# Picking the first group's rows in two parts in a transformer layer with a mixture of experts

## The chip, the cores and the metric

The kernel runs on one core of one Trainium2 chip. The metric is the time of one execution on the device in microseconds (us), as the median of several runs. The core has five engines that run their own instruction lists and wait for one another by semaphores: TensorE (PE in the profile; PEld is its loading of stationary operands), VectorE (DVE), ScalarE (ACT), GpSimd (POOL) and SyncE (SP), which here issues nearly all DMAs. A profiler on the chip records every instruction; the "granted clock" of TensorE is given as a share of its full 2.4 GHz.

## What is computed

One transformer layer on 512 rows (tokens) of 2048 features: a norm, one wide projection, three kinds of attention, an output projection added to the input, and then a mixture of experts with two levels of routing, whose output is added and normed. All is float32. The part that matters here:

```
xt = h.reshape(N, D)                                   # N = 512, D = 2048
g_prob = softmax(xt @ wg + bg); g_p, g_idx = top_k(g_prob, 1)          # one of 8 groups
e_in = the 8 expert logits of the row's own group
e_val, e_loc = top_k(e_in, 2)                          # two of its 8 experts
weight = g_p * softmax(e_val)
y[row] = sum over its two experts e of
         weight * ((silu(x @ w_gate[e]) * (x @ w_up[e])) @ w_down[e])
```

There are 64 experts, each with three matrices of 2 MB (2048x256, 2048x256, 256x2048), 403 MB in all, which are read once.

## The kernel before

Up to about 970 us the kernel does the norm, the projection and the attentions; then comes the output projection, which leaves the layer's rows in the chip's memory and, as a copy, in DRAM. From there on it goes through the 8 groups one after the other, and in each group through its 8 experts (`group(c, g, ...)`, one function of this name for each engine, with the same loop).

**Routing, ahead of the first group (lines 1209 to 1278 and 2114 to 2188).** TensorE computes the router's logits, VectorE finds each row's group and its two experts. TensorE helps with small products: a running count of the rows of each group (L1258), the rows' places in their group (`place_rows`, L1230), a running count of the chosen rows of each expert (L1270), and the slot of each row (`place_slots`, L1237). Each is followed by a step of VectorE that the next one waits for. Between them `keep_busy(n)` (L1252) runs n products of 128x128 whose result nobody reads; each shows as two records, as all float32 products do. One of these calls has n = 16 and stands ahead of the wait for the chosen experts (`chosen_ready`).

**Rows of a group and slots of an expert.** A group's rows (at most 128) are gathered by GpSimd with an indirect DMA into `xg` (two buffers). An expert has 64 slots (`CAP`). `pick` is a matrix of 128 rows by 8*64 slots that holds a 1 where row r sits in slot s of expert e; VectorE builds it in one step by comparing each row's slots with a count (`build_pick`, L2182).

**The pick.** The products of an expert need its rows turned, features by slots. That is done for four experts at a time (a half of the group, 256 columns): for each of the 16 pieces of 128 features one product of `xg` with `pick` (`pick_half`, L1297) leaves 128 features x 256 slots in a bank of the accumulator memory (PSUM), and ScalarE (even pieces, L1733) or VectorE (odd pieces, L2202) copies it to `xT`, times the norm's factor `ln2`. There are four places in PSUM for this, used in turn (`TURN4`); a pick waits until the last content of its place has been copied out. Group 0's first half is picked right after the routing, its second half after expert 3's gate and up, and the halves of later groups likewise.

**An expert.** `gate_up` multiplies its slots with the gate and up matrices, 16 pieces each, side by side in the array (L1375 and L1376), into one of two banks in turn (bank 7, `PJ`, and bank 6). Ahead of the first expert of a group it also makes eight small products with the same bank, which bring each slot's factor of the norm (the "root products", L1367). ScalarE takes the silu of the gate's half (L1753), VectorE multiplies by the up half (L2257), TensorE turns the result (L1385), and `down_product` multiplies it with the down matrix (L1400); the results are spread back over the group's rows (L1346). TensorE does this in the order: gate and up of expert e, then turn, spread and down of expert e-1. In group 0, after expert 0's gate and up, stands `place_marks` (L1245), which prepares the spreading.

**Loads.** SP issues the weights in a fixed order (`LOAD_ORDER`) into 8 slots of 2 MB. A load waits until the last user of its slot is done: `gu_done` counts experts whose gate and up are done, `down_done` those whose down product is done. The loads that follow experts 0 and 1 into their slots are cut into quarters (`load_quarters`, L753): after each quarter of gate and up TensorE signals `quarter_used`, and 2 x 512 KB go out; the fourth quarter waits for `gu_done`. Two more loads (half a matrix each, L798) wait for the gather of group 0's rows, because they overwrite the place of the rows that it reads beside.

## Time and profile before

| | us |
|---|---|
| median of 3 timed runs | 1949.46 (1948.17 to 1949.99) |
| the profiled execution's own time | 1948.38 |
| its span, first to last instruction | 1946.6 |
| TensorE busy in the span | 1871.2 (96%) |
| VectorE, ScalarE, GpSimd busy | 705.6, 584.6, 245.3 |
| DMA, all queues | 505.95 MB, mean 260 GB/s |
| mean granted clock | 0.991 |

The profile cuts the span into 40 slices of 48.7 us. TensorE shows as busy in nearly all of them, but a busy TensorE is not one at its peak, since the matmuls are pipelined and their ends modelled. The rate of the transfers has two levels: it varies between 44 and 349 GB/s up to the twenty-first slice, and is even from there on. Which of the two sets the pace of a stretch has to be read from that stretch.

### The profile page before, as it was taken

How to read it: one execution, taken by the hardware profiler on the slowest of the kernel's cores; microseconds unless marked ns; L12 is line 12 of the kernel's file. 1: busy time of each engine (PE TensorE's matmuls, PEld its weight loads, DVE VectorE, ACT ScalarE, POOL GpSimd, SP SyncE). 2: the span in 40 equal slices, each digit the busy share in tenths (PEclk: the TensorE clock that was granted, in tenths of full speed). 3: DMA queues.
4: the chain of work that ended last, by engine and by line, in shares of the span. 5: the costliest groups of instructions: out<-in, count | busy, mean ns of one | idle time of the engine just before them, and what ended most of it. 6: DMA issues, size and time to landing. Idle time of an engine off the chain costs nothing.

```text
span 1946.6 us, 28605 instructions
## 1 busy us (share of the span) xinstructions
PE 1871.2 (96%) x11936; PEld 1352.2 (69%) x11936; DVE 705.6 (36%) x1773; ACT 584.6 (30%) x1212; POOL 245.3 (13%) x208
## 2 busy tenths in 40 slices
PE   6999999999999999999999999989999899999997
PEld 6887777777777767788986666556665565656663
DVE  5331223333766668701042232322323222222222
ACT  5323333333443444422312232212212122121322
POOL 2433343433000000144100000000000000000000
PEclk9999999999999999999999999999999999999999
DMA  9554233234232232145489999999999999999995
GB/s 284 134 147 118 66 86 82 70 71 92 45 76 44 55 117 79 44 142 195 191 349 420 429 426 426 427 427 427 427 426 427 427 428 426 428 427 427 427 423 231
DMA packets 177745, 505.95 MB, mean 260 GB/s; under 512 B 52930, under 2 KB 136258, under 8 KB 151754
## 3 DMA queue, kind: packets, MB, share of 16 engines
q1 hardware_dynamic: 175306, 495.66, 66.5%
q0 software_dynamic: 2304, 8.39, 1.1%
q8 instruction: 97, 1.59, 0.3%
q14 instruction: 38, 0.31, 0.1%
HBM read 495.88 MB, written 16.53 MB: 263 GB/s over the span
## 4 chain that ended last, share of the span: by engine, by line
PE 81%; DMA 16%; ACT 1%; DVE 1%; issue 0%; SPq 0%; POOL 0%; POOLq 0%; ACTq 0%; DVEq 0%
PE banks L967 26%; PE banks L1375 13%; PE banks L1124 9%; PE banks L1400 8%; DMA x_region<-in_w_up 7%; DMA at_region<-in_w_up 7%; PE banks L1297 6%; PE banks L1376 3%; PE banks L1104 3%; PE banks L1076 2%; PE banks L1054 2%; PE banks L1346 2%; DMA ht_region<-in_w_up 2%; PE banks L1016 1%; PE banks L1215 1%; PE banks L1061 1%
## 5 line engine op out<-in xcount | busy, mean ns | idle before, releaser
L967 PE MATMUL banks<-ht_rounded,ring_rounded 128*128 128x512 f32 x1056 | 359.2, 394 | 0.7 <-ACT at_region L1538 0.7
L967 PEld LDWEIGHTS banks<-ht_rounded,ring_rounded 128*128 128x128 f32 x1056 | 195.1, 188 | 53.3 <-issue 13.8
L1375 PE MATMUL banks<-at_region,ht_region 128*64 128x256 f32 x800 | 179.0, 382 | 9.3 <-DMA at_region<-in_w_up 9.3
L864 POOL TENSOR_TENSOR ring_rounded<-ring_region,at_rounded 128x512 fp32r<-128x512 f32 (+1 forms) x92 | 115.9, 1291 | 511.3 <-ACT at_rounded L1477 511.3
L1376 PE MATMUL banks<-at_region,ht_region 128*64 128x256 f32 x768 | 175.3, 388 | 0.0
L2269 DVE SCALAR_TENSOR_TENSOR at_rounded<-banks,small,ring_rounded 128x512 fp32r<-128x512 f32 x128 | 96.1, 751 | 208.8 <-ACT ring_rounded L1763 207.9
L1763 ACT ACTIVATE ring_rounded<-banks,small 128x512 fp32r<-128x512 f32 x128 | 88.0, 687 | 241.3 <-PE banks L1400 241.3
L2262 DVE COPY consts<-banks 128x128 f32<-128x128 f32 x64 | 18.7, 292 | 388.1 <-PE banks L1385 388.1
L1375 PEld LDWEIGHTS banks<-at_region,ht_region 128*64 128x64 f32 x800 | 109.1, 138 | 67.3 <-issue 21.1
L967 PE MATMUL banks<-ht_rounded,at_rounded 128*128 128x512 f32 x352 | 142.7, 405 | 1.0 <-ACT at_region L1530 0.7
L1753 ACT ACTIVATE ring_region<-banks,consts 64x256 f32<-64x256 f32 x64 | 30.0, 469 | 364.4 <-PE banks L1376 364.1
L967 PE MATMUL banks<-mix_rounded,at_rounded 128*128 128x512 f32 x352 | 137.6, 391 | 0.0
L967 PE MATMUL banks<-mix_rounded,ring_rounded 128*128 128x512 f32 x352 | 137.6, 391 | 0.0
L864 POOL TENSOR_TENSOR ring_rounded<-ring_region,ring_rounded 128x512 fp32r<-128x512 f32 x88 | 111.1, 1294 | 198.0 <-ACT ring_rounded L1477 198.0
L1124 PE MATMUL banks<-ring_rounded,ht_rounded 128*128 128x512 f32 x384 | 129.8, 392 | 0.0
L1297 PEld LDWEIGHTS banks<-ring_region,mix_region 128*128 128x128 f32 x512 | 116.8, 306 | 15.8 <-issue 12.2
L1297 PE MATMUL banks<-ring_region,mix_region 128*128 128x256 f32 x512 | 125.1, 400 | 0.0
L1375 PE MATMUL banks<-x_region,ht_region 128*64 128x256 f32 x480 | 109.5, 388 | 12.3 <-DMA x_region<-in_w_up 12.0
L1376 PE MATMUL banks<-x_region,ht_region 128*64 128x256 f32 x512 | 117.1, 388 | 0.0
L894 POOL DMA_INDIRECT out<-mix_region,g_idx x8 | 8.0, 1005 | 833.7 <-DVE mix_region L2279 833.7
L1376 PEld LDWEIGHTS banks<-at_region,ht_region 128*64 128x64 f32 x768 | 106.4, 140 | 0.0
L1375 PEld LDWEIGHTS banks<-x_region,ht_region 128*64 128x64 f32 x480 | 66.7, 140 | 51.7 <-issue 23.5
(300 smaller groups left out, 3488.2 us busy)
## 6 DMA issues: line engine op xcount, KB each, us to landing
at_region<-in_w_gate SPq DMA_DIRECT2D x23, 2048.0 KB, 30.0
at_region<-in_w_up SPq DMA_DIRECT2D x22, 2048.0 KB, 27.6
at_region<-in_w_down SPq DMA_DIRECT2D x22, 2048.0 KB, 23.9
ring_region<-in_w_in SPq DMA_DIRECT2D x36, 1024.0 KB, 5.9
x_region<-in_w_down SPq DMA_DIRECT2D x17, 2048.0 KB, 26.6
x_region<-in_w_up SPq DMA_DIRECT2D x15, 2048.0 KB, 28.9
x_region<-in_w_gate SPq DMA_DIRECT2D x14, 2048.0 KB, 29.9
ring_region<-in_w_gate SPq DMA_DIRECT2D x9, 2048.0 KB, 32.6
```

The lines of the kernel that those rows point to most:

```text
L864: ins = nc.gpsimd.tensor_tensor(w_low[n % RING][:, ks, 0:width], ring[n % RING][:, ks, 0:width], w_high[n % 2][:, ks, 0:width].bitcast(F32 ...
L967: ins = mm(out, w[:, k, 0:width], h[:, k, :], start=k == 0 and i == 0, stop=k == KT - 1 and i == 2)
L1054: ins = mm(S[:, par, half, 0:W], q[pr][rows, cols], keys[kind == "win"][rows, 0:W], start=True, stop=True)
L1076: ins = nc.tensor.transpose(PT[:, half, kb * P:(kb + 1) * P], probs[:, n % 2, half, kb * P:(kb + 1) * P], ident)
L1104: ins = mm(o, v[:, kb, cols], pT[:, half, j * P:(j + 1) * P], start=kind == "fox" and kb == 0, stop=part != "slc" and kb == qb)
L1124: ins = mm(out, a[:, 4 * c + i, t * P:(t + 1) * P], b[:, i, :], start=first and i == 0 and k == 0, stop=last and i == 3 and k == 2)
L1297: mm(place[turn[j]][:, 0:HALF], rows[:, j, :], slots, start=True, stop=True).then_inc(picked, 1)
L1375: mm(place[0:CAP, 0:D_EXPERT], x, gate[j], start=j == 0, stop=j == KT - 1)
L1376: ins = mm(place[CAP:2 * CAP, 0:D_EXPERT], x, up[j], start=j == 0, stop=j == KT - 1)
L1400: ins = mm(PT[side * CAP:(side + 1) * CAP, m, :], hidT[:, j, :], down[:, j, (2 * m + side) * T:(2 * m + side + 1) * T], start=j == 0, stop ...
L1763: fn(y_high[:, m, :], PT[:, m, :], ACT.Copy, scale=own_weight[e8 % 2]).then_inc(y_a, 1)
L2269: v.scalar_tensor_tensor(y_low[:, m, :], PT[:, m, :], own_weight[e8 % 2], y_high[:, m, :].bitcast(F32), ALU.mult, ALU.subtract).then_inc(y ...
```

## The change

The pick of group 0's first half is cut into two parts of 128 columns: `FIRST_PARTS`, experts 0 and 1, and experts 2 and 3. The first part stands where the whole was; the second stands behind gate and up of expert 0, ahead of `place_marks`. Each part is still 16 products, one for each piece of features, each followed by a copy of ScalarE or VectorE, now of 128 columns (`pick_first`, `copy_first`). The first part has four places in PSUM, banks 6, 2, 3 and 0; the second has three, banks 2, 3 and 0. Bank 7, into which expert 0's gate and up go, is no longer among them, so that `gate_up` does not wait for it.

VectorE builds the pick matrix in three steps, with a signal (`first_picks`) after each of the first two: 128 columns, 128 columns, and the 256 of the second half.

The root products of group 0 stand behind expert 0's gate and up in place of ahead of them; expert 0's signal `gu_done` comes after them. Expert 2's gate and up wait for the second part's copies, piece by piece. The filling products ahead of the wait for the chosen experts are 11 in place of 16. The counts of picks and copies that later groups wait for grow by the 16 more (`picks_ahead`, `copies_ahead`, `half_after`). No DMA is added, removed or moved in SP's order.

```diff
@@ -225,6 +225,8 @@
 FAST_SLOTS = SLOTS + 2
 HALF = PER // 2 * CAP
 BANK_ORDER = (0, 1, 2, 3)
+FIRST_PARTS = ((0, 2 * CAP), (2 * CAP, HALF))
+FIRST_MORE = len(FIRST_PARTS) - 1
 
 TURN4 = (0, 1, 2, 3) * 3 + (0, 2, 3, 0)
 
@@ -534,8 +536,7 @@
         acc = banks[:, 0:4, :]
 
         first_banks = (banks[:, 6, :], PJ, banks[:, 2, :], banks[:, 3, :])
-        def half_places(g, h):
-            return (whole_banks if h or g else first_banks, TURN4)
+        first_places = ((banks[:, 6, :], banks[:, 2, :], banks[:, 3, :], banks[:, 0, :]), (banks[:, 2, :], banks[:, 3, :], banks[:, 0, :]))
 
         RSTD = D_EXPERT + 2 * CAP
         whole_banks = (banks[:, 6, :], PJ, PT[:, 0, :], PT[:, 1, :])
@@ -1263,7 +1269,7 @@
             ins.then_inc(cums_ready, 1)
             keep_busy(3)
             place_rows(0)
-            keep_busy(16)
+            keep_busy(11)
             pe.wait_ge(chosen_ready, 1)
             for t in range(NT):
                 for i in range(t + 1):
@@ -1276,25 +1282,39 @@
             place_slots(0)
             keep_busy(6)
 
+            first_rows = xg[0].rearrange("r (p k) -> r k p", k=KT)
+
+            def pick_first(part, j):
+                lo, hi = FIRST_PARTS[part]
+                if j == 0:
+                    pe.wait_ge(first_picks, part + 1)
+                if part == 0 and j == 0:
+                    pe.wait_ge(idx_ready, 1)
+                    pe.wait_ge(xg_in[0], 16)
+                places = first_places[part]
+                at = j - len(places)
+                if at >= 0:
+                    pe.wait_ge(xT_v if at % 2 else xT_a, part * KT // 2 + at // 2 + 1)
+                mm(places[j % len(places)][:, 0:hi - lo], first_rows[:, j, :], pick[:, lo:hi], start=True, stop=True).then_inc(picked, 1)
+
...
-                    mm(place[turn[j]][:, 0:HALF], rows[:, j, :], slots, start=True, stop=True).then_inc(picked, 1)
+                    mm(whole_banks[TURN4[j]][:, 0:HALF], rows[:, j, :], slots, start=True, stop=True).then_inc(picked, 1)
@@ -1354,18 +1374,26 @@
                 up = chunk_landed(c, g, e8, 1)
                 place = gu_bank[e8 % 2]
                 picks = e8 // (PER // 2) if fast(c) and e8 % (PER // 2) == 0 else None
-                done = copies_ahead(c, g) + (picks or 0) * (KT // 2)
+                done = copies_ahead(c, g)
+                if picks:
+                    done += half_after(g, picks)
+                if begins_all(c, g) and any(e8 * CAP == lo for lo, _ in FIRST_PARTS[1:]):
+                    picks, done = -1, KT // 2
                 if e8 == 0 and not fast(c):
                     pe.wait_ge(xT_a, done + 8)
                     pe.wait_ge(xT_v, done + 8)
-                if picks is not None:
+                if picks is not None and (g or e8 >= PER // 2):
                     i = max(j for j in range(KT) if TURN4[j] == 1)
                     pe.wait_ge(xT_v if i % 2 else xT_a, done + i // 2 + 1)
                 fence(c, g)
-                if e8 == 0:
+                def root_of_slots():
                     for i in range(PER):
-                        mm(place[0:CAP, RSTD + i * N_GROUPS:RSTD + (i + 1) * N_GROUPS], pick[:, i * CAP:(i + 1) * CAP], row_rstd,
-                           start=True, stop=True)
+                        ins = mm(place[0:CAP, RSTD + i * N_GROUPS:RSTD + (i + 1) * N_GROUPS], pick[:, i * CAP:(i + 1) * CAP],
+                                 row_rstd, start=True, stop=True)
+                    return ins
+
+                if e8 == 0 and not begins_all(c, g):
+                    root_of_slots()
                 for j in range(KT):
                     if picks is not None:
                         pe.wait_ge(xT_v if j % 2 else xT_a, done + j // 2 + 1)
@@ -1376,6 +1404,9 @@
                     ins = mm(place[CAP:2 * CAP, 0:D_EXPERT], x, up[j], start=j == 0, stop=j == KT - 1)
                     if begins_all(c, g) and e8 < len(QUARTERED) and j % 4 == 3 and j < KT - 1:
                         ins.then_inc(quarter_used, 1)
+                if e8 == 0 and begins_all(c, g):
+                    pe.wait_ge(pick_ready, 1)
+                    ins = root_of_slots()
                 ins.then_inc(gu_done, 1)
 
             def turn_hidden(c, g, e8):
@@ -1421,6 +1452,9 @@
                         continue
                     gate_up(c, g, e8)
                     if begins_all(c, g) and e8 == 0:
+                        for part in range(1, len(FIRST_PARTS)):
+                            for j in range(KT):
+                                pick_first(part, j)
                         place_marks(c)
                     if e8:
                         finish_expert(c, g, e8 - 1, begins)
@@ -1436,7 +1470,8 @@
                 else:
                     pick_rows(c, g + 1, i + b, 1 - b, False)
 
-            pick_half(0, 0)
+            for j in range(KT):
+                pick_first(0, j)
             for g in range(N_GROUPS):
                 group(0, g, g // 2, g % 2, g == 0, g == N_GROUPS - 1)
             pe.wait_ge(most_ready, 1)
@@ -1727,10 +1762,15 @@
...
+            def copy_first(part):
+                lo, hi = FIRST_PARTS[part]
+                for j in range(0, KT, 2):
+                    act.wait_ge(picked, part * KT + j + 1)
+                    fn(xT[:, 0, j, lo:hi], first_places[part][j % len(first_places[part])][:, 0:hi - lo], ACT.Copy, scale=ln2_sb[:, j:j + 1]).then_inc(xT_a, 1)
 
             def square_rows(c, g, b):
                 done = c * N_GROUPS + g
@@ -1788,7 +1828,8 @@
 
             act.wait_ge(e_diff, 1)
             fn(r_tmp[:, 4], r_tmp[:, 3], ACT.Exp).then_inc(e_exped, 1)
-            copy_half(0, 0)
+            for part in range(len(FIRST_PARTS)):
+                copy_first(part)
             for g in range(N_GROUPS):
                 group(0, g, g // 2, g % 2, g == 0, g == N_GROUPS - 1)
             act.wait_ge(most_ready, 1)
@@ -2186,7 +2227,16 @@
             v.scalar_tensor_tensor(slots1, ranks, 1.0, chosen[:], ALU.add, ALU.mult).then_inc(slots1_ready, 1)
             dve.wait_ge(slots_ready, 1)
             link(v.tensor_scalar(slot_of_row, acc[:, 0, 0:E_ALL], -1.0, None, ALU.add))
-            build_pick(0, 0)
+            v.tensor_copy(group_slots, slot_of_row[:, 0:PER]).then_inc(own_slots, 1)
+            dve.wait_ge(own_slots, 1)
+            pick_by_slots = pick.rearrange("p (e s) -> p e s", e=PER)
+            for lo, hi in FIRST_PARTS:
+                es = slice(lo // CAP, hi // CAP)
+                v.tensor_tensor(pick_by_slots[:, es, :], bcast(iota, 1, es.stop - es.start),
+                                bcast(group_slots[:, es], 2, CAP), ALU.is_equal).then_inc(first_picks, 1)
+            es = slice(HALF // CAP, PER)
+            v.tensor_tensor(pick_by_slots[:, es, :], bcast(iota, 1, PER - es.start), bcast(group_slots[:, es], 2, CAP),
+                            ALU.is_equal).then_inc(pick_ready, 1)
 
             def copy_picked(c, g, first):
                 place = first_banks if first else whole_banks
@@ -2196,13 +2246,19 @@
...
+            def copy_first(part):
+                lo, hi = FIRST_PARTS[part]
+                for j in range(1, KT, 2):
+                    dve.wait_ge(picked, part * KT + j + 1)
+                    v.tensor_scalar(xT[:, 0, j, lo:hi], first_places[part][j % len(first_places[part])][:, 0:hi - lo], ln2_sb[:, j:j + 1], None, ALU.mult)\
+                        .then_inc(xT_v, 1)
+
+            copy_first(0)
@@ -2283,6 +2339,8 @@
                 for e8 in range(PER):
                     before = None if e8 == 0 and begins else (c, g, e8 - 1) if e8 else (c, g - 1, PER - 1)
                     if begins_all(c, g) and e8 == 0:
+                        for part in range(1, len(FIRST_PARTS)):
+                            copy_first(part)
                         take_marks(c)
                     if before:
                         copy_hidT(*before)
```

TensorE from the filling products to the first row of expert 0's gate and up (L1375/L1376 before, L1403/L1404 now; `ring_region` holds the pick matrix, `mix_region` the gathered rows, `ht_region` the picked rows, and `at_region` or `x_region` weights). Before:

```order
L1252 MATMUL banks<-consts,ht_region 128x128 x16
L1270 MATMUL banks<-chosen,before_b 128x64
...
L1273 MATMUL banks<-chosen,ones_b 128x64 x4
L1252 MATMUL banks<-consts,ht_region 128x128 x4
L1237 MATMUL banks<-ring_region,at_region 128x64 x4
L1252 MATMUL banks<-consts,ht_region 128x128 x6
L1297 MATMUL banks<-ring_region,mix_region 128x256 x16
L1367 MATMUL banks<-small,ring_region 64x8 x8
L1375 MATMUL banks<-at_region,ht_region 64x256
L1376 MATMUL banks<-at_region,ht_region 64x256
```

Now:

```order
L1258 MATMUL banks<-consts,ht_region 128x128 x11
L1276 MATMUL banks<-chosen,before_b 128x64
...
L1279 MATMUL banks<-chosen,ones_b 128x64 x4
L1258 MATMUL banks<-consts,ht_region 128x128 x4
L1243 MATMUL banks<-ring_region,at_region 128x64 x4
L1258 MATMUL banks<-consts,ht_region 128x128 x6
L1298 MATMUL banks<-ring_region,mix_region 128x128 x16
L1403 MATMUL banks<-at_region,ht_region 64x256
L1404 MATMUL banks<-at_region,ht_region 64x256
```

The sixteen picks are half as wide, and gate and up follow them at once. The place behind expert 0's gate and up on TensorE, before:

```order
L1375 MATMUL banks<-at_region,ht_region 64x256
L1376 MATMUL banks<-at_region,ht_region 64x256
L1245 MATMUL banks<-at_region 64x128 x16
L1375 MATMUL banks<-at_region,ht_region 64x256
L1376 MATMUL banks<-x_region,ht_region 64x256
```

Now:

```order
L1403 MATMUL banks<-at_region,ht_region 64x256
L1404 MATMUL banks<-at_region,ht_region 64x256
L1391 MATMUL banks<-small,ring_region 64x8 x8
L1298 MATMUL banks<-ring_region,mix_region 128x128 x16
L1251 MATMUL banks<-at_region 64x128 x16
L1403 MATMUL banks<-at_region,ht_region 64x256
L1404 MATMUL banks<-x_region,ht_region 64x256
```

The root products and the second part's sixteen picks now stand between gate and up of expert 0 and the products of `place_marks`, behind which come gate and up of expert 1. On ScalarE, all 16 copies of the two parts stand ahead of the first silu (L1753 before, L1793 now):

```order
L1790 ACTIVATE r_tmp<-r_tmp 128x4
L1733 ACTIVATE ht_region<-banks,small 128x256 x8
L1751 ACTIVATE consts<-banks 64x64
L1753 ACT_TABLE_LOAD
L1753 ACTIVATE ring_region<-banks,consts 64x256 x2
```

Now:

```order
L1830 ACTIVATE r_tmp<-r_tmp 128x4
L1773 ACTIVATE ht_region<-banks,small 128x128 x16
L1791 ACTIVATE consts<-banks 64x64
L1793 ACT_TABLE_LOAD
L1793 ACTIVATE ring_region<-banks,consts 64x256 x2
```

Where eight copies of 256 columns stood, sixteen of 128 stand, and the silu of expert 0 comes behind the last of them.

## Rows read from the trace of the kernel before

**Rows 1.** The page's 40 slices: what the DMA engines moved, in GB/s.

```profile
GB/s 284 134 147 118 66 86 82 70 71 92 45 76 44 55 117 79 44 142 195 191 349 420 429 426 426 427 427 427 427 426 427 427 428 426 428 427 427 427 423 231
```

**Rows 2.** Windows: length, busy us of five engines, granted clock, DMA share, GB/s.

```profile
1060.00:1910.00 850.00, 811.90 (x5730) 519.53 (x5728) 237.86 (x530) 199.82 (x369) 14.42 (x19) 0.99 1.01 427
```

**Rows 3.** Windows: two stretches in which fewer bytes move.

```profile
996.00:1006.00 10.00, 10.00 (x112) 10.00 (x110) 4.29 (x16) 1.97 (x3) 0.00 (x0) 1.00 0.71 240
...
1053.00:1056.00 3.00, 3.00 (x22) 1.53 (x20) 0.97 (x4) 0.47 (x1) 0.00 (x0) 1.00 0.83 300
```

**Rows 4.** Timeline of SP's queue: start, length of issue, line, destination and source.

```profile
984.77 0.33 SPq L798 DMA_DIRECT2D mix_region<-in_w_up  x1
...
996.86 0.33 SPq L753 DMA_DIRECT2D at_region<-in_w_up  x1
...
1038.85 0.33 SPq L740 DMA_DIRECT2D at_region<-in_w_up  x1
1053.67 0.33 SPq L740 DMA_DIRECT2D at_region<-in_w_down  x1
```

**Rows 5.** Windows: expert 1's gate and up to the end of expert 4's.

```profile
1003.50:1053.60 50.10, 49.67 (x365) 34.18 (x360) 12.07 (x29) 9.86 (x19) 1.20 (x2) 1.00 1.02 422
```

**Rows 6.** Timeline of TensorE: filling products, and the first product on the chosen experts.

```profile
977.55 5.45 PE L1252 MATMUL banks<-consts,ht_region 128*128 128x128 f32 x32
982.83 0.19 PE L1270 MATMUL banks<-chosen,before_b 128*128 128x64 bf16 x1
```

**Rows 7.** Timeline of VectorE: the chosen experts, and the pick matrix.

```profile
980.99 0.42 DVE L2166 TENSOR_TENSOR chosen<-g_tmp 128x256 bf16<-128x256 f32 x1
...
985.72 0.69 DVE L2182 TENSOR_TENSOR ring_region<-consts,small 128x512 f32<-128x512 f32 x1
```

**Rows 8.** Chain that ended last: start, us, products of 128x128 (turns L1177, filling L1252).

```profile
963.98 1.84 PE banks L1177 x16
...
983.40 0.97 PE banks L1252 x8
```

**Rows 9.** Windows: ahead of and in the filling products (the clock is third from last).

```profile
976.00:977.00 1.00, 0.47 (x5) 0.36 (x4) 0.97 (x3) 0.00 (x0) 0.00 (x0) 1.00 1.00 426
978.00:981.00 3.00, 3.00 (x16) 3.00 (x16) 2.56 (x17) 0.23 (x1) 1.41 (x2) 0.50 0.99 426
```

**Rows 10.** Timeline of TensorE: last filling products, picks, root products, first turn.

```profile
985.05 1.56 PE L1252 MATMUL banks<-consts,ht_region 128*128 128x128 f32 x12
986.47 7.54 PE L1297 MATMUL banks<-ring_region,mix_region 128*128 128x256 f32 x32
993.94 1.04 PE L1367 MATMUL banks<-small,ring_region 128*64 128x8 f32 x15
...
1010.58 0.45 PE L1385 MATMUL banks<-consts,ring_region 64*128 64x64 f32 x2
```

**Rows 11.** Timelines of ScalarE and VectorE: copies of picks 10, 12, 13 and 15.

```profile
991.76 0.47 ACT L1733 ACTIVATE ht_region<-banks,small 128x256 f32<-128x256 f32 x1 [0.42 <-PE banks L1297]
992.65 0.47 ACT L1733 ACTIVATE ht_region<-banks,small 128x256 f32<-128x256 f32 x1 [0.42 <-PE banks L1297]
...
993.14 0.48 DVE L2202 TENSOR_SCALAR ht_region<-banks,small 128x256 f32<-128x256 f32 x1 [0.45 <-PE banks L1297]
994.05 0.48 DVE L2202 TENSOR_SCALAR ht_region<-banks,small 128x256 f32<-128x256 f32 x1 [0.43 <-PE banks L1297]
```

**Rows 12.** Groups by form: copies out of PSUM, count, busy us, mean ns.

```profile
L1612 ACT ACTIVATE at_region<-banks 128x128 f32<-128x128 f32 x24 | 6.7, 279 | 0.5 <-PE banks L1076 0.5
L1612 ACT ACTIVATE at_region<-banks 128x256 f32<-128x256 f32 x16 | 6.1, 380 | 2.1 <-PE banks L1076 2.1
...
L2012 DVE COPY at_region<-banks 128x256 f32<-128x256 f32 x12 | 5.0, 420 | 16.8 <-PE banks L1104 16.4 <-PE banks L1076 0.3
L2012 DVE COPY at_region<-banks 128x128 f32<-128x128 f32 x4 | 1.2, 292 | 1.8 <-PE banks L1104 1.3 <-PE banks L1093 0.5
```

**Rows 13.** Timeline of VectorE: expert 0's product of silu and up.

```profile
1004.31 0.42 DVE L2257 TENSOR_TENSOR ring_region<-ring_region,banks 64x256 f32<-64x256 f32 x1
```

More of the change, by code:

```diff
@@ L553, in picks_ahead, with half_after @@
         def picks_ahead(c, g):
-            return g * 2 * KT if fast(c) else (c * N_GROUPS + g) * KT + N_GROUPS * KT
+            return g * 2 * KT + (FIRST_MORE * KT if g else 0) if fast(c) else (c * N_GROUPS + g) * KT + N_GROUPS * KT + FIRST_MORE * KT
         def copies_ahead(c, g):
-            return g * KT if fast(c) else (c * N_GROUPS + g) * (KT // 2) + N_GROUPS * KT // 2
+            return g * KT + (FIRST_MORE * KT // 2 if g else 0) if fast(c) else ((c * N_GROUPS + g) * (KT // 2) + N_GROUPS * KT // 2
+                                                                               + FIRST_MORE * KT // 2)
+        def half_after(g, h):
+            return h * (KT // 2) + (FIRST_MORE * KT // 2 if h and not g else 0)
         def begins_all(c, g):
@@ L1277, in _ @@
             keep_busy(6)
+            first_rows = xg[0].rearrange("r (p k) -> r k p", k=KT)
[11 more added lines that the diff above has]
+                mm(places[j % len(places)][:, 0:hi - lo], first_rows[:, j, :], pick[:, lo:hi], start=True, stop=True).then_inc(picked, 1)
             def pick_half(g, h):
                 pe.wait_ge(pick_ready, g + 1)
[L1282 to L1284 removed]
                 rows = xg[g % 2].rearrange("r (p k) -> r k p", k=KT)
+                if not h:
+                    pe.wait_ge(xg_in[g % 2], g // 2 * 16 + 16)
                 for j in range(KT):
[L1287 removed]
+                    if j == TURN4.index(0):
                         pe.wait_ge(hid_done, g * PER + PER // 2 * h)
[L1289 removed]
+                    if j == TURN4.index(2):
                         pe.wait_ge(y_v, 2 * (g * PER + PER // 2 * h - 1) - 1)
[L1291 removed]
+                    if j == TURN4.index(3):
                         pe.wait_ge(y_v, 2 * (g * PER + PER // 2 * h - 1))
[L1293 removed]
+                    i = last_user(TURN4, j)
                     if i is not None:
[L1295 removed]
+                        pe.wait_ge(xT_v if i % 2 else xT_a, copies_ahead(0, g) + half_after(g, h) + i // 2 + 1)
                     slots = pick[:, h * HALF:(h + 1) * HALF]
[L1297 removed]
+                    mm(whole_banks[TURN4[j]][:, 0:HALF], rows[:, j, :], slots, start=True, stop=True).then_inc(picked, 1)
             def pick_rows(c, g, i, b, first):
@@ L1729, in copy_half @@
             def copy_half(g, h):
-                place, turn = half_places(g, h)
                 for j in range(0, KT, 2):
-                    act.wait_ge(picked, picks_ahead(0, g) + h * KT + j + 1)
-                    fn(xT[:, 0, j, :], place[turn[j]][:, 0:HALF], ACT.Copy, scale=ln2_sb[:, j:j + 1]).then_inc(xT_a, 1)
+                    act.wait_ge(picked, picks_ahead(0, g) + 2 * half_after(g, h) + j + 1)
+                    fn(xT[:, 0, j, :], whole_banks[TURN4[j]][:, 0:HALF], ACT.Copy, scale=ln2_sb[:, j:j + 1]).then_inc(xT_a, 1)
+            def copy_first(part):
[3 more added lines that the diff above has]
+                    fn(xT[:, 0, j, lo:hi], first_places[part][j % len(first_places[part])][:, 0:hi - lo], ACT.Copy, scale=ln2_sb[:, j:j + 1]).then_inc(xT_a, 1)
             def square_rows(c, g, b):
```

15 lines of the change are left out of this document (3 added, 12 removed).

## The prediction

> **What bounds the kernel now.** I read the slices of the page first [rows 1]: from the twenty-second of the 40 on, the DMA engines move 420 to 429 GB/s up to the last two, so the second half of the kernel, where the weights of 64 experts stream in, is paced by the transfers. The window table makes it exact: 427 GB/s over 1060 to 1910 us, at a DMA share of 1.01 [rows 2]. No matmul in that stretch is worth anything by itself. Such a program ends when its bytes have been moved, so the end is set by the last moment before it at which the DMA queue ran dry and by what then refilled it. Everything that the change touches lies ahead of 1060 us, so I looked there for dry places. There are two: 996 to 1006 us at 240 GB/s, and 1053 to 1056 us at 300 GB/s [rows 3]. Against 427 they lose (427-240)*10/427 = 4.4 us and (427-300)*3/427 = 0.9 us.
>
> The second is the later one, and so the one that counts. SP's queue shows why it is there [rows 4]: after the load issued at 1038.85 us nothing is issued until 1053.67 us, where a load waits for expert 4's gate and up to free a slot. TensorE set that moment: it was busy 49.67 of the 50.1 us from 1003.5 to 1053.6 [rows 5], a fixed list of products with a pick of 256 columns among them. The first dry place is earlier: SP could issue the first quarter loads only at 996.86 us [rows 4], when a quarter of expert 0's products had been done. What is moved sooner there makes the queue run dry sooner before 1053, unless TensorE also arrives sooner at 1053.67. So I ask of each edit: when does TensorE finish expert 4's gate and up? The end of the kernel moves by that amount, as far as it is later; as far as it is earlier, by no more than the 0.9 us that are idle there, before a load ahead of it takes over.
>
> **The change part by part.** *Eleven filling products in place of sixteen.* Each is two records in the trace. The 32 records of the sixteen start at 977.55 us and the products that wait for the chosen experts start at 982.83 [rows 6], though the row that they wait for was written by 980.99 + 0.42 = 981.41 us [rows 7]: TensorE is late by 1.4 us. At full clock a record takes 0.97/8 = 0.12 us [rows 8] or a little less, and the last ones of the row run at it, so ten records fewer give 1.1 us: start at 981.7, still behind 981.41. All that follows on that chain (ranks, slots, the row -1, the pick matrix) moves with it, as each step waits for the one ahead. The picks also wait for the gathered rows; SP, which waits for the same, issued at 984.77 [rows 4], and the picks would start at 986.47 - 1.1 = 985.4, so the gather does not get in the way. Term: **-1.1 us**.
>
> What hid the filling products' length? In this execution the granted clock was 0.50, the lower of its two levels (1.2 GHz), from 978 to 981 us; in the microsecond 976 to 977 ahead of it TensorE was busy for 0.47 us only [rows 9]. At full clock 32 records of 0.115 us end at 981.2, ahead of 981.41, and then the five products cost nothing before and save nothing now. The Trainium skill, "TensorE: Matmul & The Clock Gate", section "What's actually happening", says that the point at which the clock steps is not tied to the kernel's own timing and shifts from run to run; by that the term lies anywhere between 0 and -1.1 us in the timed runs, and the sum below would be up to 1.1 us higher. One profile can't show it; I keep it as a rival.
>
> *The pick in parts of 128 columns.* Before, 16 picks of 256 columns ran from 986.47 to 993.94 = 7.47 us [rows 10], a pace of 0.44 us per pick that TensorE itself set. A pick of 128 columns is two records again; turns of 128x128 take 1.84/16 = 0.115 us each [rows 8], so 0.23 us per pick if nothing is waited for. But each pick's place must be copied out before it is used again, and with half the columns this loop becomes the slower one. The trace has it measured for a place used again three picks later: the copies of picks 10 and 13 start at 991.76 and 993.14, those of 12 and 15 at 992.65 and 994.05 [rows 11], that is 1.38 and 1.40 us for one turn, of which 0.47 to 0.48 is the copy and 0.91 the picking with its hand-overs. For 128 columns the pick's two records are 2*0.105 us shorter (0.44/2 against 0.115), which leaves 0.70. The copy: ScalarE's copies without a scale go from 380 to 279 ns with the columns halved, VectorE's from 420 to 292 [rows 12], so 0.47 and 0.48 us become about 0.37 and 0.355; I take 0.36. One turn is then 1.06 us. It does not halve, since most of it is fixed.
>
> The first part has four places: picks 4, 8 and 12 each wait for one turn, 3*1.06 + 4*0.23 = 4.1 us. The second has three: five turns and one pick, 5*1.06 + 0.23 = 5.5 us. Together 9.6 against 7.47: **+2.1 us** of TensorE. The bounds: if nothing waited, 32*0.23 = 7.4 us, which is -0.1; if a turn were as long as it is for 256 columns, 8*1.39 + 1.2 = 12.3 us, which is +4.8. I stand near the middle, as the two measured pieces (fixed hand-overs, shorter copies) give it. The second part sits between gate and up of expert 0 and the marks, ahead of gate and up of expert 1, so nothing hides its waits on TensorE.
>
> *Everything else.* The eight root products are moved behind expert 0's gate and up, same count, no sum. They delay that expert's completion signal by about 0.9 us, and with it the last quarter load, which has a backlog ahead of it. On ScalarE the silu of expert 0 (with a table load) now stands behind the copies of the second part, and on VectorE the product with it as well, at 1004.31 before [rows 13]; who waits for that is the turn of the hidden rows at 1010.58 [rows 10], behind gate and up of expert 1. Those 6 us are the cover: the second part ends some 1 us after the old gate and up of expert 0 did, so the product comes 1 to 2 us later. Without that cover its delay would be TensorE's. The pick matrix is built in three pieces in place of one of 0.69 us [rows 7]; the first is there some 0.4 us sooner, but the last filling products start at 985.05 [rows 10], run for 12*0.12 us and end just when the whole matrix used to be there, so I count nothing. The DMAs are the same, in the same order; the quarter loads of expert 0 go out some 5 us sooner (gate and up of expert 0 begins at 985.4 + 4.1 us, where the root products stood at 993.94), and that is where the data of 996 to 1006 us comes sooner. It is given back at 1053, for the reason above.
>
> **The sum.** -1.1 + 2.1 = **+1.0 us** at the issue that stood at 1053.67 us, so the queue stands dry about 1 us longer, and the end moves by that. The profiled execution took 1948.38 us (span 1946.6); the sum is 1949.4. The median of the three timed runs is 1949.46, 1.1 above it, so against the median I say **1950.5 us**. A difference of 0.2% (3.9 us) is about what a measurement of this kernel can tell from no change; the forecast lies well inside.
>
> **The rivals.**
>
> *The clock does not fall in the timed runs* (0.18). The filling products then cost nothing before, the term of -1.1 goes, and the sum is +2.1: 1951.6 us. For it: the page's rule above. Against it: the products ahead of the fall are the same in each run.
>
> *The copies keep up* (0.16). If a turn is some 0.3 us shorter than I worked out, TensorE sets the pace in both parts and reaches expert 4 about 1.0 us sooner. Then the 0.9 us of idle transfer go: 1948.6 us. For it: busy time of a copy may overstate when its place is free. Against it: the measured turn of 1.39 us has that already in it.
>
> *The clock falls behind the second part: slower* (0.05). Its place is 997 to 1003 us, where TensorE would work 0.23 of every 0.35 us. At 0.50 a product takes twice its time, so the fall of 978 to 981 us cost half of its 3 us, 1.5 us. One such stretch makes 1952.0; it takes two, over the marks and the start of expert 1, to be 1.0 + 3.1 = 4.1 us slower, 1953.6, beyond 0.2%. Against it: over 1060 to 1910 us, where TensorE often waits for data, the mean clock is 0.99 [rows 2].
>
> *What is regained at 996 to 1006 us counts after all: faster* (0.03). If the issue at 1053.67 were not what starves the queue, 4.4 us earlier transfers would bring 1945.1 us, just over 0.2%. It decides if the queue still holds over 2 MB at that moment. Against it: the dip to 300 GB/s lies exactly there.
>
> *How the numbers follow.* The forecast itself (a net of +0.3 to +1.8 us) has 0.54; 0.04 is left for what I have not seen. The timed runs scatter by 1.8 us, so the median may be off by some tenths. From the "copies keep up" case less a few tenths to the "no fall" case with a turn 0.1 us longer gives 1948.3 to 1952.4. Faster by over 0.2%: 0.03. Slower: 0.05. The rest, 0.92, is within.
>
> **What would show it.** In the changed trace: the products on the chosen experts start near 981.7; the first picks start near 985.4 and take 4.1 us, with copies in turns of about 1.06 us; expert 0's gate and up start near 989.5; the second picks take about 5.5 us; gate and up of expert 1 start near 1004.5 instead of 1003.5; 996 to 1003 us is filled with transfers, with a short dry place when expert 1's first quarter is awaited, near 1006 to 1008; the issue of 1053.67 comes at about 1054.7 and the dry place there is 1 to 3 us longer. I am wrong if the queue is not dry there, if the second part takes under 4 us or over 7, or if the clock stands at 0.5 anywhere between 985 and 1010 us.

## The result, and the profile after

The changed kernel takes 1955.47 us (median of 8 runs, 1953.76 to 1959.31), the kernel before 1949.72 us beside it (8 runs, 1947.28 to 1952.44). The ratio is 1.0032, with a 95% interval of 1.0021 to 1.0043: 5.8 us slower, where 1.0 us was forecast, and 3 us above the upper end of the range, 1952.4. The profiled execution took 1955.41 us (span 1953.6), 7.03 us more than that of before, at the same mean granted clock of 0.991.

The issue on which the prediction hung its sum is the first to look at. This is SP's queue in the changed kernel (start, us, line, buffers); it answers to [rows 4]:

```profile
995.37 0.33 SPq L759 DMA_DIRECT2D at_region<-in_w_up  x1
...
1012.24 0.33 SPq L759 DMA_DIRECT2D at_region<-in_w_gate  x1
...
1045.57 0.33 SPq L746 DMA_DIRECT2D at_region<-in_w_up  x1
1060.39 0.33 SPq L746 DMA_DIRECT2D at_region<-in_w_down  x1
```

The load that waits for expert 4's gate and up goes out at 1060.39 in place of 1053.67, which is 6.72 us later, and the kernel ends 7.03 us later. The first quarter load goes out 1.5 us sooner than before (995.37 against 996.86), and that brought nothing. The windows show the same (length, busy us of each engine, granted clock third from last, DMA share, GB/s); they answer to [rows 2, 3]:

```profile
996.00:1006.00 10.00, 10.00 (x79) 8.51 (x76) 4.16 (x16) 1.84 (x5) 0.00 (x0) 1.00 0.97 342
1008.00:1014.00 6.00, 6.00 (x71) 4.66 (x72) 1.31 (x5) 2.22 (x4) 0.00 (x0) 1.00 0.22 60
1053.00:1056.00 3.00, 3.00 (x28) 1.92 (x28) 0.48 (x1) 0.37 (x1) 0.00 (x0) 1.00 1.02 437
1060.00:1064.00 4.00, 4.00 (x26) 1.82 (x24) 0.97 (x4) 0.79 (x2) 0.00 (x0) 1.00 0.78 250
1067.00:1917.00 850.00, 815.15 (x5728) 522.80 (x5724) 237.56 (x528) 199.83 (x369) 14.41 (x19) 0.99 1.01 427
```

The old dry place at 996 to 1006 us has risen from 240 to 342 GB/s; a new one stands at 1008 to 1014 us, with 60 GB/s; the late one has moved from 1053 to 1060, and behind it the transfers run at full rate again (438 GB/s over 1064 to 1066 us, 427 from 1067 on, as before). So nothing was lost behind 1064 us. The time lies on TensorE, ahead of the issue. Its timeline (start, us), which answers to [rows 6, 10]:

```profile
978.52 4.33 PE L1258 MATMUL banks<-consts,ht_region 128*128 128x128 f32 x22
982.69 0.19 PE L1276 MATMUL banks<-chosen,before_b 128*128 128x64 bf16 x1
...
986.30 7.15 PE L1298 MATMUL banks<-ring_region,mix_region 128*128 128x128 f32 x32
1000.34 1.05 PE L1391 MATMUL banks<-small,ring_region 128*64 128x8 f32 x16
1001.32 7.25 PE L1298 MATMUL banks<-ring_region,mix_region 128*128 128x128 f32 x32
1008.50 1.97 PE L1251 MATMUL banks<-at_region 128*64 128x128 f32 x32
1017.30 0.45 PE L1416 MATMUL banks<-consts,ring_region 64*128 64x64 f32 x2
```

The filling products now take 4.17 us up to the products on the chosen experts, against 982.83 - 977.55 = 5.28 before: 1.11 us less, as forecast. But each part of the pick takes as long as the whole did. 16 picks of 128 columns take 7.15 and 7.25 us, 16 of 256 columns took 7.54. From the first pick to the issue it is 1060.39 - 986.30 = 74.09 us, against 1053.67 - 986.47 = 67.20 before: 6.89 more, and 7.15 + 7.25 - 7.54 is 6.86. That is all of it.

Who set that pace? Not the copies. These are the copies of the parts by form (count, busy us, mean ns; then the idle time ahead of them and who ended it), the ScalarE ones and the VectorE ones, and under them two copies from ScalarE's timeline:

```profile
L1773 ACT ACTIVATE ht_region<-banks,small 128x128 f32<-128x128 f32 x16 | 5.9, 367 | 19.9 <-PE banks L1298 19.9
...
L2258 DVE TENSOR_SCALAR ht_region<-banks,small 128x128 f32<-128x128 f32 x16 | 5.6, 351 | 11.7 <-PE banks L1298 11.7
...
1002.93 0.37 ACT L1773 ACTIVATE ht_region<-banks,small 128x128 f32<-128x128 f32 x1 [0.50 <-PE banks L1298]
1003.80 0.37 ACT L1773 ACTIVATE ht_region<-banks,small 128x128 f32<-128x128 f32 x1 [0.51 <-PE banks L1298]
```

The copies shrank to about the forecast lengths (0.367 and 0.351 us for 0.37 and 0.355), and both engines wait 0.5 us for TensorE ahead of each. TensorE waits for neither: one copy of ScalarE comes every 0.87 us, a pick every 0.44, and the second part with three places runs at the pace of the first with four. What is left is TensorE itself, and there the loads of the stationary operand stand out:

```profile
L1298 PEld LDWEIGHTS banks<-ring_region,mix_region 128*128 128x128 f32 x64 | 14.1, 312 | 0.0
...
L1258 PEld LDWEIGHTS banks<-consts,ht_region 128*128 128x128 f32 x3 | 0.4, 192 | 0.0
```

Loads of the same 128x128 shape take 312 ns for the pick and 192 for the filling products. The pick's loads are busy for 14.1 of its 14.4 us. They read `first_rows[:, j, :]`, which takes every 16th float of a gathered row, so a step of 64 bytes. The kernel before had the same two numbers in its page and in the group of the router's products:

```profile
L1297 PEld LDWEIGHTS banks<-ring_region,mix_region 128*128 128x128 f32 x512 | 116.8, 306 | 15.8 <-issue 12.2
...
L1215 PEld LDWEIGHTS banks<-at_region,ht_region 128*128 128x128 f32 x45 | 5.2, 192 | 0.0
```

There the long load hid behind 256 moving columns, which need about the same time: expert 0's gate products in the changed kernel, with as many columns and loads of 0.14 us, start every 0.215 us, and the wide picks of before come at 0.22 us for each of their records ([rows 11]: 0.89 us from copy to copy, two picks of two records). With 128 columns the load stands free.

The turns of 128x128, from which the prediction has its 0.115 us a record, show less of this, though they read at the same step (`x_sb[:, t, 4 * j + i:D:KT]`). They are transpositions, one record each. In the kernel before, the load of such a turn takes 197 ns, that of a transposition of floats in a row (`diff_rows[:, t, u * P:(u + 1) * P]`) 140:

```profile
L1177 PEld LDWEIGHTS banks<-consts,mix_region 128*128 128x128 f32 x64 | 7.6, 197 | 0.1
...
L1185 PEld LDWEIGHTS banks<-consts,x_region 128*128 128x128 f32 x16 | 1.7, 140 | 0.2 <-issue 0.2
```

### The profile page after: what moved, and what is told of

It reads as the page before. It is cut to its first block, busy times and chain, and to the rows that moved or that the text cites. A ratio compares the mean times of both kernels' runs of the same rounds, so it can differ in the third digit from the quotient of the medians.

```text
span 1953.6 us, 28652 instructions
## 1 busy us (share of the span) xinstructions
PE 1881.4 (96%) x11958; PEld 1358.3 (70%) x11958; DVE 706.7 (36%) x1783; ACT 586.5 (30%) x1220; POOL 245.4 (13%) x208
## 4 chain that ended last, share of the span: by engine, by line
PE 81%; DMA 16%; ACT 1%; DVE 1%; issue 0%; SPq 0%; POOL 0%; POOLq 0%; ACTq 0%; DVEq 0%
PE banks L973 26%; PE banks L1403 13%; PE banks L1130 9%; PE banks L1431 8%; DMA x_region<-in_w_up 7%; DMA at_region<-in_w_up 7%; PE banks L1317 6%; PE banks L1110 3%; PE banks L1082 2%; PE banks L1060 2%; PE banks L1404 2%; PE banks L1366 2%; DMA ht_region<-in_w_up 2%; PE banks L1022 1%; PE banks L1298 1%; PE banks L1221 1%
## 5 line engine op out<-in xcount | busy, mean ns | idle before, releaser
L1403 PE MATMUL banks<-at_region,ht_region 128*64 128x256 f32 x800 | 182.3, 387 | 9.7 <-DMA at_region<-in_w_up 9.7
L1404 PE MATMUL banks<-at_region,ht_region 128*64 128x256 f32 x768 | 178.6, 393 | 0.0
L1403 PEld LDWEIGHTS banks<-at_region,ht_region 128*64 128x64 f32 x800 | 110.8, 140 | 73.9 <-issue 22.6
L1793 ACT ACTIVATE ring_region<-banks,consts 64x256 f32<-64x256 f32 x64 | 30.0, 469 | 365.1 <-PE banks L1404 364.8
L1317 PEld LDWEIGHTS banks<-ring_region,mix_region 128*128 128x128 f32 x480 | 109.5, 306 | 15.7 <-issue 12.2
L1403 PE MATMUL banks<-x_region,ht_region 128*64 128x256 f32 x480 | 109.6, 388 | 9.2 <-DMA x_region<-in_w_up 8.2
L1317 PE MATMUL banks<-ring_region,mix_region 128*128 128x256 f32 x480 | 117.6, 400 | 0.0
L1404 PE MATMUL banks<-x_region,ht_region 128*64 128x256 f32 x512 | 117.2, 389 | 0.0
L1404 PEld LDWEIGHTS banks<-at_region,ht_region 128*64 128x64 f32 x768 | 108.2, 142 | 0.0
L1403 PEld LDWEIGHTS banks<-x_region,ht_region 128*64 128x64 f32 x480 | 66.8, 140 | 47.4 <-issue 19.7
```

Of the source, the lines that this page charges most:

```text
L1317: mm(whole_banks[TURN4[j]][:, 0:HALF], rows[:, j, :], slots, start=True, stop=True).then_inc(picked, 1)
L1403: mm(place[0:CAP, 0:D_EXPERT], x, gate[j], start=j == 0, stop=j == KT - 1)
L1404: ins = mm(place[CAP:2 * CAP, 0:D_EXPERT], x, up[j], start=j == 0, stop=j == KT - 1)
```

## The experiments

**Theory 1.** The pace of the parts is set by the stationary load with its step of 64 bytes, and the end of the kernel follows TensorE's arrival at the issue of 1053.67. **Rivals:** the copies or the number of places set the pace; the new dry place at 1008 to 1014 us is what costs; or the later root products, the three steps of the pick matrix or the filling products do.

**One part.** All of the change except the cut:

```
-FIRST_PARTS = ((0, 2 * CAP), (2 * CAP, HALF))
+FIRST_PARTS = ((0, HALF),)
```

> The changed kernel with FIRST_PARTS of one part of 256 columns: the split is undone, the eleven filling products, the later root products and the places without bank 7 stay. Theory 1 (the split itself costs, since a pick takes 0.44 us at 128 columns as at 256): the 16 picks take about 7.1 us once, TensorE reaches the end of expert 4's gate and up 7.0 us sooner than in the changed kernel and about 1.3 us sooner than before, and the time is 1.0 us below before, at 1948.7 (ratio 0.9995). Rival (the cost sits in the later root products or in the fewer filling products): the time stays 4 us or more above before.

Measured: 1948.6 us (11 runs, 1947.62 to 1950.58), a ratio of 0.9995 (0.9986 to 1.0004) to before. The 16 picks of 256 columns and the issue in its profile:

```profile
986.18 7.37 PE L1298 MATMUL banks<-ring_region,mix_region 128*128 128x256 f32 x32
...
1053.21 0.33 SPq L746 DMA_DIRECT2D at_region<-in_w_down  x1
```

So the cut carries the whole loss; root products, matrix steps and filling products carry none of it that can be measured.

**Even rows.** The stationary operand of each pick is read as 128 floats in a row:

```
-mm(..., first_rows[:, j, :], pick[:, lo:hi], ...)
+mm(..., xg[0][:, j * P:(j + 1) * P], pick[:, lo:hi], ...)
```

> The changed kernel, but both parts of the first pick take 128 neighbouring features of each row as the stationary operand in place of every sixteenth one; the rows of xT then belong to other weights, so the first four experts' results are not the reference's. Theory 1 (loading the stationary operand with a step of 64 bytes sets the pace of a pick): the two parts fall from 7.1 us each to the 4.1 and 5.5 us that the prediction worked out from the copies, TensorE arrives 4.5 us sooner at expert 4, and the time is about 1951.0, 1.2 above before. Rival (the hand-over with the copies, or signals and waits of each pick, set 0.44 us): both parts stay at 7.1 us and the time at 1955.5.

Measured: 1950.08 us (11 runs, 1948.53 to 1952.09), ratio 1.0003 (0.9994 to 1.0012). TensorE's timeline in this kernel, and its loads by form:

```profile
987.06 3.90 PE L1298 MATMUL banks<-ring_region,mix_region 128*128 128x128 f32 x32
998.82 5.19 PE L1298 MATMUL banks<-ring_region,mix_region 128*128 128x128 f32 x32
...
L1298 PEld LDWEIGHTS banks<-ring_region,mix_region 128*128 128x128 f32 x64 | 7.9, 190 | 1.0 <-ACT ht_region L1773 0.6 <-DVE ht_region L2258 0.4
```

With nothing changed but the step, the load falls from 312 to 190 ns and the parts from 7.15 and 7.25 to 3.90 and 5.19 us. Now, and only now, TensorE waits for copies, 0.6 us for ScalarE's and 0.4 for VectorE's, and the part with three places is the slower one. These are nearly the 4.1 and 5.5 us of the forecast, and the time is nearly the forecast one of 1950.5. The load's step is the cause; the copy loop stood behind it.

**Steps of 2 and 4.** To see on what the load time depends, the first part reads at a step of 2 floats and the second at a step of 4:

```
+step = (2, 4)[part]
+at = j // step * step * P + j % step
-mm(..., first_rows[:, j, :], pick[:, lo:hi], ...)
+mm(..., xg[0][:, at:at + step * P - step + 1:step], pick[:, lo:hi], ...)
```

> The changed kernel with the rows' operand of the first part read at a step of 2 floats and that of the second at a step of 4, in place of 16 (other features than the reference's are picked, so the first four experts' results are not the reference's). At a step of 1 the two parts took 3.90 and 5.19 us, at 16 they took 7.15 and 7.25. Theory A (what counts is whether neighbouring elements share a stretch of 16 bytes): a step of 4 costs as much as one of 16, so the second part takes 7.2 us again, its loads about 310 ns; a step of 2 lies between, the first part 3.9 to 5.5 us. Theory B (the cost grows with the step up to 16): the second part stays near its 5.2 us, the first at 3.9. Theory C (any step but 1 is slow): 7.15 and 7.25. The end follows: 1948.7 less what TensorE arrives sooner than at 7.2 us each, that is 1955.4 under C and 1950 to 1953 under A and B.

Measured, in one execution: 1952.79 us. TensorE's timeline, and the loads by form, first in a window around the first part, then around the second:

```profile
986.27 3.99 PE L1300 MATMUL banks<-ring_region,mix_region 128*128 128x128 f32 x32
...
998.12 7.73 PE L1300 MATMUL banks<-ring_region,mix_region 128*128 128x128 f32 x32
...
L1300 PEld LDWEIGHTS banks<-ring_region,mix_region 128*128 128x128 f32 x32 | 3.9, 196 | 0.0
...
L1300 PEld LDWEIGHTS banks<-ring_region,mix_region 128*128 128x128 f32 x32 | 7.5, 328 | 0.0
```

A step of 2 floats (8 bytes) is as quick as none, 196 ns; a step of 4 (16 bytes) is as slow as 16, 328 ns. Theory A holds, B and C fall. The Trainium skill, "Advanced Engine Details and Errata", section "Memory Cachelines", says that the on-chip memory SBUF works in lines of 16 bytes and that at least two accesses must hit a line for full speed. The rows agree: at a step of 2 there are two floats to a line (196 ns), at 4 and 16 one (328 and 312 ns). Why 4 is even a little slower than 16 (7.73 against 7.25 us) this one execution does not tell.

**Late part.** The second part behind gate and up of expert 1 in place of expert 0, on all three engines, so that expert 1's quarter loads are not held up:

```
 gate_up(c, g, e8)
 if begins_all(c, g) and e8 == 0:
+    place_marks(c)
+if begins_all(c, g) and e8 == 1:
     for part in range(1, len(FIRST_PARTS)):
         ...
-    place_marks(c)
```

> The changed kernel with the second part one expert later: behind gate and up of expert 1, on TensorE, ScalarE and VectorE; nothing else moved. Expert 1's quarter loads go out about 7 us sooner, so the dry place of 1008 to 1014 us (5.2 us of transfers lost) is mostly filled, while TensorE does the same work before expert 4. Theory 1 (the end follows TensorE's arrival at expert 4): the time stays at 1955.5 within 0.7 us, and the dry place near 1061 us grows from 1.7 to 6 us or so. Rival (the loss is the dry place at 1008 to 1014 us): the time falls by 4 to 5 us, to about 1951.

Measured: 1954.68 us (10 runs, 1953.22 to 1956.98), ratio 1.0029 (1.002 to 1.0039). Its windows:

```profile
1008.00:1014.00 6.00, 6.00 (x43) 5.62 (x38) 0.95 (x3) 1.10 (x3) 0.00 (x0) 1.00 1.02 412
1014.00:1057.00 43.00, 42.57 (x277) 28.89 (x278) 13.06 (x32) 11.06 (x22) 1.20 (x2) 1.00 0.90 366
...
1060.00:1064.00 4.00, 4.00 (x28) 1.97 (x26) 0.97 (x4) 0.47 (x1) 0.00 (x0) 1.00 0.57 168
```

The dry place of the changed kernel is filled, 412 GB/s in place of 60, and the kernel is as slow as the changed one. What came sooner is given back: 366 GB/s over 1014 to 1057 us, where the changed kernel has 399, and 168 GB/s over 1060 to 1064, where it has 250. TensorE's work is the same, the issue comes at 1061.11, and the end follows that. But most of the hole is not where the expectation put it: at 1060 to 1064 us (427-168)*4/427 = 2.4 us are lost in place of 6. Most of the rest has moved to 1020 to 1023 us (46 GB/s) and 1029 to 1032 (153), since no load goes out between 1011.32 and 1022.58 us: the next one waits for expert 0's down product, now behind the second part. So this run shows that the place at 1008 to 1014 us is not what costs, but not by itself that dry places ahead of the issue cost nothing; for that see one part under the table.

**Early double and late double.** The kernel before, with some picks made twice: those of group 0's first half, ahead of the issue, or those of group 3's first half, where transfers set the pace. The same 16 extra picks in both, by the pace of 0.44 us about 7.0 us of TensorE (early double shows 74.21 - 67.20 = 7.01 up to the issue):

```
+if (g, h) == (0, 0):        # late double: (3, 0)
+    mm(place[turn[j]][:, 0:HALF], rows[:, j, :], slots, start=True, stop=True)
 mm(place[turn[j]][:, 0:HALF], rows[:, j, :], slots, start=True, stop=True).then_inc(picked, 1)
```

> The kernel before, with each of the first 16 picks (256 columns) made twice into the same place: 32 more records, nothing else. Theory 1 (any TensorE time ahead of expert 4 counts in full): 7.0 us more of TensorE, the load that stood at 1053.67 us is issued near 1060.7, and the time is 7 us above before, at 1956.7 (ratio 1.0036). Rival (later loads with a backlog absorb it): 0 to 3 us above before.

> The kernel before, with each of the 16 picks of group 3's first half made twice, which adds TensorE work of 16 * 0.44 = 7.0 us in the stretch where the transfers run at 427 GB/s. Theory (behind 1060 us TensorE's time is paid by the transfers; only its arrival at the issue that stood at 1053.67 us moves the end): the end does not move, 1948.8 within a microsecond, and the doubled picks are followed by shorter waits for data. Rival (any 7 us of TensorE work is 7 us of the kernel, as early_double and the changed kernel could also be read): 1956.

Measured: early double 1956.83 us (5 runs, 1955.06 to 1957.51), ratio 1.0035 (1.0022 to 1.0049); late double 1948.97 us (11 runs, 1947.03 to 1950.25), ratio 1.0004 (0.9995 to 1.0013). The place decides. These are late double's windows around its doubled picks and over the whole transfer-bound stretch; the latter answers to [rows 2], where TensorE was busy 811.90 us:

```profile
1324.00:1331.00 7.00, 7.00 (x32) 6.37 (x29) 2.77 (x5) 2.11 (x4) 0.00 (x0) 1.00 1.01 428
1331.00:1338.00 7.00, 7.00 (x33) 7.00 (x33) 1.94 (x4) 1.90 (x4) 0.00 (x0) 1.00 1.01 431
...
1060.00:1910.00 850.00, 818.19 (x5762) 525.45 (x5760) 237.21 (x527) 199.85 (x369) 14.42 (x19) 0.99 1.01 427
```

TensorE is busy for 6.3 us more in the stretch than before (3.5 more than in fill 11 below, which has 814.69 without extra picks), the rate stays at 427 GB/s, and the end does not move.

**Fewer filling products alone.** The kernel before with `keep_busy(11)` in place of `keep_busy(16)`:

> The kernel before with 11 filling products in place of 16, and nothing else. Theory (the five products were on TensorE's path only where the granted clock falls to 0.50 in them): in a profile with such a fall the picks start 1.1 us sooner and the load of 1053.67 is issued at most 1.1 us sooner; in one without, nothing moves. Over the timed runs 1948.0 to 1948.8, a ratio between 0.9994 and 1. Rival (the filling products also keep the clock up, and with fewer of them it falls later, in the slots or the picks): the picks take over 8 us and the end is 1 to 3 us later.

Measured: 1948.7 us (11 runs, 1945.92 to 1950.08), ratio 0.9999 (0.999 to 1.0008). TensorE's timeline in fill 11, and under it the same place in late double, which has the 16:

```profile
976.89 2.70 PE L1252 MATMUL banks<-consts,ht_region 128*128 128x128 f32 x22
980.81 0.20 PE L1270 MATMUL banks<-chosen,before_b 128*128 128x64 bf16 x1 [1.22 <-DVE chosen L2166]
...
977.12 3.82 PE L1252 MATMUL banks<-consts,ht_region 128*128 128x128 f32 x32
981.04 0.20 PE L1270 MATMUL banks<-chosen,before_b 128*128 128x64 bf16 x1
```

In both the products on the chosen experts start 3.92 us after the first filling product: at full clock the five products cost nothing, since TensorE then waits 1.2 us for VectorE instead. The picks take 7.54 us as before, so the fewer products did not bring the clock down. The rival's 3 us are excluded; its 1 us and the theory's -1.1 at most both lie within the interval (-1.9 to +1.6 us), so the timed runs do not tell those apart.

**All executions in one table.** Arrival is the issue of the load that waits for expert 4's gate and up, in the profiled execution; all in us.

| kernel | picks of group 0's first half | first pick to arrival | arrival | end | end - arrival |
|---|---|---|---|---|---|
| before | 7.5 | 67.20 | 1053.67 | 1948.38 | 894.71 |
| fill 11 | 7.5 | 67.20 | 1051.66 | 1946.68 | 895.02 |
| late double | 7.5 | 67.21 | 1051.90 | 1947.03 | 895.13 |
| one part | 7.4 | 67.03 | 1053.21 | 1948.69 | 895.48 |
| even rows | 3.9 + 5.2 | 68.78 | 1055.84 | 1950.80 | 894.96 |
| steps 2, 4 | 4.0 + 7.7 | 71.43 | 1057.70 | 1952.79 | 895.09 |
| changed | 7.2 + 7.3 | 74.09 | 1060.39 | 1955.41 | 895.02 |
| late part | 7.2 + 7.3 | 74.00 | 1061.11 | 1956.04 | 894.93 |
| early double | 14.5 | 74.21 | 1061.17 | 1956.92 | 895.75 |

The arrival moves by 9.5 us from row to row, the last column by 1.0: the end is the arrival plus 895 us, whatever was done about the transfers ahead of it. One part beside before shows it most plainly: over 996 to 1006 us it moves 338 GB/s where before moved 240, the queue is drier for it over 1053 to 1056 us (218 GB/s for 300), and the two end together.

## Why the prediction was wrong, step by step

- **What bounds the kernel: right.** The end follows TensorE's arrival at the issue of 1053.67, and sooner transfers at 996 to 1006 us are given back (table; one part, early double, late double). The bound for a sooner arrival, at most 0.9 us, was not tested: where the arrival is sooner in the table, the kernel's earlier part was sooner too.
- **The pick in parts, +2.1 us: wrong, it was +6.9.** The step that failed is the pace of "0.23 us per pick if nothing is waited for". It was taken from turns of 128x128, two records for one pick. But a turn is a transposition and no product. It reads its rows at the same step of 64 bytes, and still its load takes only 197 ns and a record 0.115 us. The pick's own load takes 306 ns at this step, where a product's load takes 192 in a row, and comes every 0.22 us with 128 columns as with 256; a pick of 128 columns has two of them, 0.44 us. The kernel before had these rows in its page and its trace; I took the duration by shape and looked neither at the kind of instruction nor at the pick's own load. Why the step costs a product's load 114 ns and a transposition's 57, no run tells. So the upper bound of +4.8 us was none: it let only the copies limit the part. A bound that assumes nothing would have been "each half as long as the whole", 7.5 us more, and the result lies near it.
- **The turn of 1.06 us for the copies: near in size, by luck, and not what decides.** Copies took 367 and 351 ns for the 0.37 and 0.355 us forecast, and even rows, where the load is quick, took 3.90 and 5.19 us for the 4.1 and 5.5 forecast; there two turns are 1.88 us (ScalarE's copies at 1000.51 and 1002.39), 0.94 each. But the rows that gave the turn do not show the loop: in [rows 11] each copy waits 0.42 to 0.45 us for TensorE, so 1.38 us is three picks at TensorE's own pace (0.44 to 0.45 us each from copy to copy; the 7.47/16 that the prediction put beside its 0.44 is 0.47), and only an upper bound for a turn. So the answer to the rival "the copies keep up", that the measured turn "has that already in it", did not hold. In the changed kernel the copies did keep up, only TensorE was slower and not faster.
- **Eleven filling products, -1.1 us: right in the profiled execution, and nothing at full clock.** The changed kernel's profile has the granted clock at 0.50 over 979 to 982 us, as before had it over 978 to 981 [rows 9], and gains 1.11 us. That both profiles compared have the fall is luck: in the seven others the clock is 1.00 there, and the five products cost nothing (fill 11 beside late double). Ahead of the fall TensorE was busy 0.48 us of a microsecond in the changed kernel and in one part alike, and only the former fell. So the rival "the clock does not fall" was the commoner case, where I gave it 0.18; I argued that equal work ahead means an equal clock. The Trainium skill, "TensorE: Matmul & The Clock Gate", section "What's actually happening", says that the point at which the clock steps is not tied to the kernel's start. The nine profiles fit that, two with the fall and seven without, but they do not show what brings it down.
- **The cover of expert 0's silu, the root products, the matrix in three steps: right.** ScalarE's silu starts at 1009.95 and VectorE's product at 1011.03 in the changed kernel. That is 6.7 us later than [rows 13], where 1 to 2 were forecast, but the turn that needs them is as much later: it starts at 1017.30, right behind gate and up of expert 1. One part has the root products and the fewer filling products too, and is as fast as before.
- **"A short dry place near 1006 to 1008 us": there, but longer,** 1008 to 1014 us, since the second part took 7.25 us for 5.5. The first quarter load went out 1.5 us sooner in place of some 5, mostly since the first part took 7.15 us for 4.1. The mark that I set for being wrong, a second part of over 7 us, was met.

Against before's profile the sum now reads: 0.97 us from the part ahead of the filling products (they start at 978.52 for 977.55; executions differ by that much), -1.11 for the filling, +6.9 for the parts: 6.7 us at the issue, and 7.0 at the end. In the timed runs it is 5.8, with an interval of 4.1 to 8.4.

## What to carry to other kernels

Cutting a product into narrower ones halves its moving columns, but not its stationary loads: before counting on half the time, read the load's own row (PEld) and compare it with other loads of the same shape and kind (a transposition's is another kind), for a long one may lie hidden behind the wide product. Where transfers set the pace to the end, find the last issue that an engine holds up; in this kernel work of that engine ahead of it counted in full, and work behind it and sooner transfers ahead of it for nothing.

## What the hardware showed

- Loading the float32 stationary operand of a 128x128 product took 190 ns with its floats in a row, 196 at a step of 2, 328 at a step of 4 and 312 at a step of 16; the products of 128 columns that wait for nothing else then follow one another every 0.12, 0.12, 0.24 and 0.22 us. The load of a float32 transposition of 128x128 took 140 ns in a row (L1185) and 197 at a step of 16 (L1177).
- The granted clock fell to 0.50 in the filling products in two profiled executions of nine, with the same work ahead of them. What brings it down there stays open.
